# Halving the first transfers and moving the output norms and their turns in a two-block fp32 kernel

## The chip, the cores and the metric

One core of one Trainium2 chip runs the whole program. The metric is device time in microseconds (us), from launch to end, as the median of repeated runs. The engines are TensorE (PE in the rows, PEld for its weight loads), VectorE (DVE), ScalarE (ACT), GpSimd (POOL) and SyncE (SP), each with its own instruction queue, in order, and tied to the others by semaphores. A row's number after L is a line of the kernel.

## The reference

512 tokens of width 1024 pass, in fp32, through three stages, of which this study touches the start of the first and one part of the last.

```python
for i in range(2):                      # first block
    m = even_mixer(x) if i % 2 == 0 else odd_mixer(x)
    x = layer_norm(ALPHA * x + m)
    x = layer_norm(ALPHA * x + square(relu(x @ w_up)) @ w_down)
    x = x + sigmoid(x @ w_gate + b) * (p @ w_proj)
# even_mixer begins with h = x @ w_in; its first 384 columns are c_q
h = rmsnorm(x)                          # second block
q, k, v, g, a, c_b, c_c, c_h = split(h @ w_in_2)
log_a = log_sigmoid(a @ w_gate_up + b_gate) / 16
b = cumsum(log_a) within chunks of 64
q_i, k_i, k_s = q*exp(b), k*exp(-b), k*exp(b_last - b)
o = tril(q_i k_i^T) v + q_i state_prev       # 4 heads, 8 chunks
state = exp(b_last) * state_prev + k_s^T v
o_gla = rmsnorm(o, per head) * g_norm * silu(g)
o_conv = c_b * causal_conv3(c_c * c_h)
x = x + concat(o_gla, o_conv) @ w_out
x = x + (silu(h2 @ w_g) * (h2 @ w_u)) @ w_down ; return rmsnorm(x)
```

## The kernel before

**Products.** Every fp32 operand is held as two parts, H (rounded) and L (the rest), and a product is three matmuls: H with H, H with L, L with H (`mm3`). Weights come as one stream of 303 chunks of 128x1024 (512 KB). SP loads each into one of four raw buffers (`RW`); `cut` on POOL copies it to its H part `WH` (L486) and subtracts to get its L part `WL` (L489), into one of two slots; TensorE waits for `lo_split` before a chunk and raises `chunk_used` after it, which lets POOL cut two chunks on. One chunk against 512 tokens is two steps of k with 12 matmuls each.

**The opening.** ACT's queue loads the transposed input `XS` in four pieces of 512 KB, two steps of k each, and casts each to `XTH`; DVE subtracts to `XTL` (L1207). POOL cuts chunks 0 to 3. TensorE runs 28 matmuls on a tile of ones (`occupy`, operand `IDLE`), whose results nobody reads, then for each of eight k: four token tiles of 384 columns and one tile of 512 columns, three matmuls each, the three parts of a product next to each other. The matmuls of `occupy` keep TensorE at work while it would wait.

**The mixer of the second block.** Its tokens are taken in T = 4 tiles. For tile t the steps on TensorE are `score` (12 matmuls and two turns of `KK`, into banks 4 and 5), `key_values` (banks 6 and 7), `output` (bank 6) and `turn_output` (four turns of `OT` into bank 5, so that it can be multiplied with `w_out`). They are put by hand between the half-chunks of three `features` calls (24 matmuls between two steps), which compute the projections `c_b`... as columns of features in banks 0 to 3. `f(t)` is `turn_output(t)` followed by 11 matmuls of `occupy`, except for the last; `score(0)` has 14 ahead of it.

DVE runs, in order: the three products `QI`, `KI`, `KK` with `QK` (L1628); `operands(0)` (the parts of the two operands, L1634 to L1637, which raise `gla_ops`); then for each t `cut_scores(t)` (mask and parts of the scores, parts of the turned keys, L1645 to L1651, and four casts of the query parts, L1655 and L1656), `operands(t+1)`, `norm_output(t-1)` (L1682 to L1695, with a square root on ACT in the middle), `states(t)` (L1663 to L1673: the parts of the state, twice, and its update, `gla_states` after the second pair of parts), and `output_lo(t-1)` (L1701). After the loop come the convolution's product, its first tap, `norm_output(3)`, the second tap, `output_lo(3)` and the third.

ACT copies finished banks (`copy_banks`), the mixer's outputs (`output_out`), takes the square roots (`output_std`) and casts the turned outputs (`output_hi`), in the order of a loop over t.

The last turn, `f(3)`, stands before the last 24 matmuls of the third `features` call; the product with `w_out` follows and waits for `out_cut` 4.

Of the kernel before, what the change touches and what calls it, by code (L numbers as in the profile page):

```python
# [21 lines left out]
F32 = mybir.dt.float32  # L22
F32R = mybir.dt.float32r
ALU = mybir.AluOpType
ACT = mybir.ActivationFunctionType

P = 128
# [142 lines left out]
def program(nc, d, out):  # L170
    ctx = ExitStack()
    with ctx:
# [166 lines left out]

        landed = [sem(f"raw_landed{j}") for j in range(RAW)]  # L340
        hi_split = sem("hi_split")
        lo_split = sem("lo_split")
# [72 lines left out]
        mix_out = sem("mix_out")  # L415
        gla_ops = sem("gla_operands")
        gla_scored = sem("gla_scored")
        gla_cut = sem("gla_cut")
# [27 lines left out]
        def _(sp):  # L446
# [4 lines left out]

            for j in range(RAW):
                if j >= 2:
                    sp.wait_ge(xs_landed[j - 2], 16)
                load(0, j)
# [22 lines left out]
        def _(pool):  # L478
# [42 lines left out]
            own(pool.memset(ONE[:, :], 1.0))  # L521
            for j in range(RAW):
                cut(0, j)
            over_chunks(pool, RAW, FIRST["out0"], cut)
# [62 lines left out]
        def _(pe):  # L587
# [19 lines left out]

            def features(c, bank, r=0, new=0, freed=None, steps=None):

                columns, k_tiles = (0, P, 2 * P, 3 * P), KD
                for k in range(k_tiles):
                    cc, u = c + k // 2, UNIT * (k % 2)
                    if new:
                        pe.wait_ge(xt_ready, KD * (new - 1) + k + 1)
                    if k % 2 == 0:
                        chunk(cc, r)
                    for m, col in enumerate(columns):
                        if freed is not None and k == 0:  # L620
                            pe.wait_ge(mix_out, freed + m + 1)
                        w = slice(u + col, u + col + P)
                        x = mm3(PS[:, bank + m, :], WH[:, cc % WS, w], WL[:, cc % WS, w],
                                XTH[:, k, :], XTL[:, k, :], k == 0, k == k_tiles - 1)
                    if k % 2:
                        x.then_inc(chunk_used, 1)
                        if steps:
                            for step, t in steps[k // 2]:
                                step(t)
# [289 lines left out]
            pe.wait_ge(idle_made, 1)  # L919
            occupy(1, 28)  # L920
            c = FIRST["cq"]
            for k in range(KD):
                cc, u = c + k // 2, UNIT * (k % 2)
# [188 lines left out]
            def score(t):  # L1112


                if t == 0:
                    occupy(6, 14)
                pe.wait_ge(gla_ops, t + 1)
                if t >= 2:
                    pe.wait_ge(out_cut, t - 1)
                for h in range(GLA_H):  # L1120
                    rows, p = slice(DK * (h % 2), DK * (h % 2 + 1)), h // 2
                    mm3(PS[:, 4 + h % 2, P * p:P * (p + 1)], KIH[rows, p, :], KIL[rows, p, :],
                        QIH[rows, p, :], QIL[rows, p, :], True, True)
                for p in range(2):
                    x = pe.transpose(PS[:, 5, P * (p + 2):P * (p + 3)], KK[:, p, t * P:(t + 1) * P], IDENT[:, :])
# [15 lines left out]
            def output(t):  # L1141

                pe.wait_ge(gla_states, t + 1)
                for p in range(2):
                    w = slice(2 * DV * p, 2 * DV * (p + 1))
# [9 lines left out]
            def turn_output(t):  # L1155

                pe.wait_ge(out_gated, t + 1)
                if t < T - 1:
                    pe.wait_ge(gla_cut, t + 2)
                for f in range(GLA_H):  # L1160
                    x = pe.transpose(PS[:, 5, f * P:(f + 1) * P], OT[:, t, f * P:(f + 1) * P], IDENT[:, :])
                x.then_inc(out_turned, 1)

            s, v, o = score, key_values, output

            def f(t):

                turn_output(t)
                if t < T - 1:
                    occupy(4, 11)  # L1170

            features(c + 12, 0, freed=0, steps=[[], [(s, 0)], [(v, 0)], [(o, 0), (s, 1)]])
            features(c + 16, 0, freed=4, steps=[[(v, 1)], [(f, 0), (o, 1), (s, 2)], [(v, 2)],
                                                [(f, 1), (o, 2), (s, 3)]])
            features(c + 20, 0, freed=8, steps=[[(v, 3)], [(f, 2), (o, 3)], [(f, 3)], []])
            pe.wait_ge(out_cut, 4)
# [14 lines left out]
        def _(ve):  # L1191
# [11 lines left out]
            ve.memset(EPS[:, 1:2], RMS_EPS)  # L1203
            for j in range(4):
                w = slice(2 * j, 2 * j + 2)
                ve.wait_ge(xt_hi, j + 1)
                ve.tensor_tensor(XTL[:, w, :], XS[:, w, :], XTH[:, w, :].bitcast(F32), SUB).then_inc(xt_ready, 2)  # L1207
# [417 lines left out]

            for n, (o, src) in enumerate(((QI, QG), (KI, KG), (KK, KG))):
                ve.wait_ge(gla_act, n + 2)
# [11 lines left out]
            def cut_scores(t):  # L1639
# [11 lines left out]
                ve.tensor_tensor(SML[:, :], SMF[:, :], SMH[:, :].bitcast(F32), SUB).then_inc(gla_cut, 1)  # L1651
                ve.wait_ge(gla_ops, t + 1)
                for e in range(2):
                    k = slice(GCH * e, GCH * (e + 1))
                    ve.tensor_copy(QEH[:, e, :, k], QIH[:, :, k].bitcast(F32))  # L1655
                    x = ve.tensor_copy(QEL[:, e, :, k], QIL[:, :, k].bitcast(F32))  # L1656
                own(x)

# [44 lines left out]

            operands(0)
            for t in range(T):
                cut_scores(t)
                if t < T - 1:
                    operands(t + 1)
                if t:
                    norm_output(t - 1)  # L1710
                states(t)
                if t:
                    output_lo(t - 1)
            ve.wait_ge(mix_out, 12)
            own(ve.tensor_tensor(U[:, :, 2:S + 2], U[:, :, 2:S + 2], CV[:, :, :], M))

# [9 lines left out]
            own(x)  # L1726
            norm_output(T - 1)
            taps(1)
            output_lo(T - 1)
            taps(2)  # L1730
# [13 lines left out]
        def _(act):  # L1744
# [5 lines left out]

            for j in range(4):
                w = slice(2 * j, 2 * j + 2)
                load(XS[:, w, :], d["xt"][:, w, :], xs_landed[j])
            for j in range(4):
                w = slice(2 * j, 2 * j + 2)
                act.wait_ge(xs_landed[j], 16)
                act.copy(XTH[:, w, :], XS[:, w, :]).then_inc(xt_hi, 1)
            load(ONEHOT[:, :], d["onehot"], const_landed)
            load(REL[:, :], d["rel"], const_landed)
# [210 lines left out]
            def copy_banks(o, chunks):  # L1970

                act.wait_ge(chunk_used, chunks)
                for m in range(4):
                    act.copy(o[:, m, :], PS[:, m, :]).then_inc(mix_out, 1)

            def output_out(t):
                act.wait_ge(gla_out, t + 1)
# [10 lines left out]

            c = FIRST["gla"]
            copy_banks(CV, c + 16)  # L1990
            for t in range(T):
                output_out(t)
                output_std(t)
                output_hi(t)
                if t == 1:
                    copy_banks(U[:, :, 2:S + 2], c + 20)
            copy_banks(QK, c + 24)
# [140 lines left out]
```

## Time and profile before

| | us |
|---|---|
| median of 3 runs (2023.68 to 2025.64) | 2023.72 |
| profiled execution, its own time | 2025.68 |
| its span | 2023.9 |
| busy PE / PEld / DVE / ACT / POOL | 1972.5 / 1634.2 / 875.3 / 316.2 / 1272.6 |
| mean granted clock of TensorE | 0.995 |

The span is the time between the first and the last recorded instruction. Matmuls are pipelined: the start of one to the start of the next is what it costs, and its own duration in a row is longer. A matmul of the tile of ones counts as busy. Idle time of an engine is shown ahead of an instruction in brackets, with what ended it.

### The profile page before, as it was taken

How to read it: one execution, taken by the hardware profiler on the slowest of the kernel's cores; microseconds unless marked ns; L12 is line 12 of the kernel's file. 1: busy time of each engine (PE TensorE's matmuls, PEld its weight loads, DVE VectorE, ACT ScalarE, POOL GpSimd, SP SyncE). 2: the span in 40 equal slices, each digit the busy share in tenths (PEclk: the TensorE clock that was granted, in tenths of full speed). 3: DMA queues.
4: the chain of work that ended last, by engine and by line, in shares of the span. 5: the costliest groups of instructions: out<-in, count | busy, mean ns of one | idle time of the engine just before them, and what ended most of it. 6: DMA issues, size and time to landing. Idle time of an engine off the chain costs nothing.

```text
span 2023.9 us, 24676 instructions
## 1 busy us (share of the span) xinstructions
PE 1972.5 (97%) x9253; PEld 1634.2 (81%) x9253; DVE 875.3 (43%) x1215; ACT 316.2 (16%) x601; POOL 1272.6 (63%) x831
## 2 busy tenths in 40 slices
PE   9999999999999999999999999999999899999998
PEld 8778778888887878888788888877887778888886
DVE  3367282343338610472732343377368740000234
ACT  1247120000003100362300000033111130000001
POOL 5488566667775547775566677765553456666675
PEclk9999999999999999999999999999999999999999
DMA  6310323333332223212233333322221223323332
GB/s 213 125 43 1 94 94 95 101 96 114 95 102 83 84 84 95 68 55 76 73 115 102 94 115 95 102 77 80 76 84 53 63 84 95 103 94 93 96 101 73
DMA packets 53410, 181.32 MB, mean 90 GB/s; under 512 B 6552, under 2 KB 9290, under 8 KB 53210
## 3 DMA queue, kind: packets, MB, share of 16 engines
q1 hardware_dynamic: 46512, 165.17, 26.4%
q10 hardware_dynamic: 6826, 15.11, 2.2%
q8 instruction: 54, 0.88, 0.2%
q14 instruction: 18, 0.15, 0.0%
HBM read 176.56 MB, written 3.70 MB: 89 GB/s over the span
## 4 chain that ended last, share of the span: by engine, by line
PE 85%; DVE 9%; POOL 3%; ACT 1%; issue 1%; DMA 0%; POOLq 0%; DVEq 0%
PE PS L589 83%; PE PS L748 1%; POOL WL L489 1%; PE PS L825 1%; DVE OT L1693 1%; DVE STL L1664 1%; POOL WH L486 1%; DVE X L1509 0%; DVE X L1408 0%; DVE PS L1391 0%; POOL PB L518 0%; DVE PTL L1334 0%; DVE ST L1673 0%; POOL AQL L495 0%; POOL AKL L495 0%
## 5 line engine op out<-in xcount | busy, mean ns | idle before, releaser
L489 POOL TENSOR_TENSOR WL<-RW,WH 128x1024 fp32r<-128x1024 f32 x303 | 767.7, 2534 | 25.3
L486 POOL TENSOR_SCALAR WH<-RW 128x1024 fp32r<-128x1024 f32 x303 | 351.4, 1160 | 669.3 <-PE PS L589 640.7
L589 PE MATMUL PS<-XTH,WH 128*128 128x512 f32 x1168 | 458.3, 392 | 2.5 <-DVE XTL L1441 1.6
L589 PE MATMUL PS<-XTL,WH 128*128 128x512 f32 x1168 | 456.2, 391 | 0.0
L589 PE MATMUL PS<-XTH,WL 128*128 128x512 f32 x1168 | 456.0, 390 | 0.0
L589 PE MATMUL PS<-WL,HSH 128*128 128x512 f32 x688 | 267.6, 390 | 2.1 <-POOL WL L489 2.1
L589 PE MATMUL PS<-WH,HSH 128*128 128x512 f32 x688 | 267.7, 389 | 0.0
L589 PE MATMUL PS<-WH,HSL 128*128 128x512 f32 x688 | 267.7, 389 | 0.0
L589 PEld LDWEIGHTS PS<-XTH,WH 128*128 128x128 f32 x1168 | 220.2, 189 | 51.1 <-DVE XTL L1441 3.6
L589 PEld LDWEIGHTS PS<-XTH,WL 128*128 128x128 f32 x1168 | 220.0, 188 | 46.0
L589 PEld LDWEIGHTS PS<-XTL,WH 128*128 128x128 f32 x1168 | 220.1, 188 | 44.8
L589 PE MATMUL PS<-WH,XTH 128*128 128x512 f32 (+1 forms) x480 | 184.7, 385 | 4.4 <-DVE SG L1521 1.8
L589 PE MATMUL PS<-WL,XTH 128*128 128x512 f32 (+1 forms) x480 | 183.4, 383 | 0.5 <-POOL WL L489 0.5
L589 PE MATMUL PS<-WH,XTL 128*128 128x512 f32 (+1 forms) x480 | 183.5, 382 | 0.0
L1494 DVE CAST HSH<-HT 128x512 fp32r (+1 forms) x86 | 40.3, 468 | 273.9 <-PE PS L589 273.1
L589 PEld LDWEIGHTS PS<-WL,HSH 128*128 128x128 f32 x688 | 128.9, 188 | 30.0 <-POOL WL L489 3.4
L589 PEld LDWEIGHTS PS<-WH,HSH 128*128 128x128 f32 x688 | 129.1, 188 | 27.0
L589 PEld LDWEIGHTS PS<-WH,HSL 128*128 128x128 f32 x688 | 129.1, 188 | 26.8
L1495 DVE TENSOR_TENSOR HSL<-HT,HSH 128x512 fp32r<-128x512 f32 x86 | 124.0, 1442 | 3.0
L1456 DVE TENSOR_SCALAR HT<-PS 128x2048 f32 (+1 forms) x16 | 36.7, 2292 | 201.2 <-PE PS L589 200.5
L589 PEld LDWEIGHTS PS<-WH,XTH 128*128 128x128 f32 x480 | 90.1, 188 | 26.0 <-issue 8.3
L1478 DVE TENSOR_TENSOR HT<-PS,GT 128x1024 f32 (+1 forms) x11 | 13.5, 1225 | 214.7 <-ACT GT L2008 214.7
(313 smaller groups left out, 2346.0 us busy)
## 6 DMA issues: line engine op xcount, KB each, us to landing
RW<-stream SPq DMA_DIRECT2D x303, 512.0 KB, 3.6
BC<-gate_rows SPq DMA_DIRECT2D x16, 256.0 KB, 3.2
G<-gain_rows ACTq DMA_DIRECT2D x5, 512.0 KB, 3.5
XS<-xt ACTq DMA_DIRECT2D x4, 512.0 KB, 8.0
X<-x ACTq DMA_DIRECT2D x1, 2048.0 KB, 11.9
G<-bias_vecs ACTq DMA_DIRECT2D x4, 512.0 KB, 5.1
out<-X SPq DMA_DIRECT2D x4, 512.0 KB, 2.6
bias_rows<-QM ACTq DMA_DIRECT2D x1, 1536.0 KB, 6.8
```

What stands on the lines that cost most here:

```text
L486: pool.tensor_scalar(WH[:, j % WS, :], RW[:, j % RAW, :], 1.0, 1.0, ALU.mult, ALU.mult).then_inc(hi_split, 1)
L489: pool.tensor_tensor(WL[:, j % WS, :], RW[:, j % RAW, :], WH[:, j % WS, :].bitcast(F32), ALU.subtract).then_inc(lo_split, 1)
L589: return pe.matmul(o, a, b, start=start, stop=stop)
L748: x = pe.transpose(PSF[:, o:o + P], probs(h)[:, p:p + P], IDENT[:, :])
L825: x = pe.transpose(PS[:, 2 * t + k // 4, P * (k % 4):P * (k % 4 + 1)], src[:, k * P:(k + 1) * P], IDENT[:, :])
L1456: ve.tensor_scalar(h, PS[:, 4 * (g % 2):4 * (g % 2) + 4, :], 0.0, None, MAX).then_inc(relued, 1)
L1478: ve.tensor_tensor(h, PS[:, bank + 2:bank + 4, :], GT[:, :, :], M).then_inc(relued, 1)
L1494: own(ve.tensor_copy(HSH[:, k % 2, :], h))
L1495: ve.tensor_tensor(HSL[:, k % 2, :], h, HSH[:, k % 2, :].bitcast(F32), SUB).then_inc(hs_ready, 1)
L1664: x = ve.tensor_tensor(STL[:, e, :, :], ST[:, :, :], STH[:, e, :, :].bitcast(F32), SUB)
L1693: x = ve.scalar_tensor_tensor(OT[:, t, w], OT[:, t, w], ORS[:, h:h + 1], GN[:, :], M, M)
```

## The change

1. The first weight chunk and the first piece of `XS` are each loaded as two transfers of half the size. ACT, POOL and DVE cut them in halves.
2. The first four k on TensorE are ordered by part: all five H-with-H products of a k (or of k 2 and 3 together), then those with `WL`, then those with `XTL`. The matmuls of `occupy` ahead are 18 in place of 28.
3. The H part of chunk 2 is cast by ACT, ahead of ACT's loads of constants; POOL only subtracts.
4. In the mixer, `KK` is multiplied behind `operands(0)`, with a semaphore of its own (`gla_keys`) that `score(0)` waits for ahead of its two turns. `occupy` ahead of `score(0)` has 6 matmuls in place of 14, and the 33 behind the turns are gone.
5. The four casts of the query parts go from DVE to ACT (`query_parts`); DVE waits for them (`gla_parts`) before it writes the next operands.
6. On DVE `norm_output(t-1)` comes behind `states(t)`, and `output_lo` one tile later. `norm_output(3)` and `output_lo(2)` come ahead of the convolution, and `output_lo(3)` inside its product, which is now four instructions.
7. On TensorE each turn comes one or more steps later; turns 0 to 2 no longer stand directly ahead of `output`, and turn 3 stands after k = 6 of the third `features` call, ahead of its last 12 matmuls. A turn now also waits for the `output_lo` of the tile before.
8. ACT's order is written out by hand.

```diff
@@ -449,7 +454,10 @@
-            for j in range(RAW):
+            sp.dma_start(RW[:, 0, 0:UNIT], d["stream"][0][:, 0:UNIT]).then_inc(half_landed, 16)
+            sp.dma_start(RW[:, 0, UNIT:], d["stream"][0][:, UNIT:]).then_inc(landed[0], 16)
+            for j in range(1, RAW):
@@ -519,8 +527,18 @@
-            for j in range(RAW):
-                cut(0, j)
+            for half, (here, done) in enumerate(((half_landed, half_lo), (landed[0], lo_split))):
+                w = slice(UNIT * half, UNIT * (half + 1))
+                pool.wait_ge(here, 16)
+                pool.tensor_scalar(WH[:, 0, w], RW[:, 0, w], 1.0, 1.0, ALU.mult, ALU.mult).then_inc(hi_split, 1)
+                pool.wait_ge(hi_split, half + 1)
+                pool.tensor_tensor(WL[:, 0, w], RW[:, 0, w], WH[:, 0, w].bitcast(F32),
+                                   ALU.subtract).then_inc(done, 1)
+            cut(0, 1)
+            pool.wait_ge(hi_split, 6)
+            pool.tensor_tensor(WL[:, 0, :], RW[:, 2, :], WH[:, 0, :].bitcast(F32),
+                               ALU.subtract).then_inc(lo_split, 1)
+            cut(0, 3)
@@ -622,6 +640,8 @@
+                    if k == 6 and inner:
+                        inner[0](inner[1])
@@ -917,9 +937,36 @@
-            occupy(1, 28)
+            occupy(1, 18)
             c = FIRST["cq"]
-            for k in range(KD):
+            def opening(k, a, b, first):
+                u = UNIT * (k % 2)
+                for t in range(T):
+                    ts = slice(t * P, (t + 1) * P)
+                    mm(PS[:, 4 + t, 0:Q_LORA], a[:, k, ts], b[:, k // 2, u:u + Q_LORA], first, False)
+                w = slice(u + Q_LORA, u + UNIT)
+                return mm(PS[:, 0, :], b[:, k // 2, w], a[:, k, :], first, False)
+            for ks in ((0,), (1,), (2, 3)):
+                for k in ks:
+                    pe.wait_ge(xt_hi, (1, 2, 3, 3)[k])
+                    pe.wait_ge(hi_split, (1, 2, 4, 4)[k])
+                    opening(k, XTH, WH, k == 0)
+                for k in ks:
+                    if k == 0:
+                        pe.wait_ge(half_lo, 1)
+                    else:
+                        chunk(k // 2)
+                    opening(k, XTH, WL, False)
+                for k in ks:
+                    pe.wait_ge(xt_ready, k + 1)
+                    x = opening(k, XTL, WH, False)
+                if k % 2:
+                    x.then_inc(chunk_used, 1)
+            for k in range(4, KD):
@@ -1113,14 +1160,16 @@
-                    occupy(6, 14)
+                    occupy(6, 6)
                 pe.wait_ge(gla_ops, t + 1)
-                if t >= 2:
-                    pe.wait_ge(out_cut, t - 1)
+                if t >= 3:
+                    pe.wait_ge(out_cut, t - 2)
...
+                if t == 0:
+                    pe.wait_ge(gla_keys, 1)
@@ -1141,6 +1190,7 @@
+                pe.wait_ge(gla_parts, t + 1)
@@ -1156,23 +1206,20 @@
-                    pe.wait_ge(gla_cut, t + 2)
+                    pe.wait_ge(gla_cut, min(t + 3, T))
+                if t:
+                    pe.wait_ge(out_cut, t)
...
-            s, v, o = score, key_values, output
-            def f(t):
-                turn_output(t)
-                if t < T - 1:
-                    occupy(4, 11)
+            s, v, o, f = score, key_values, output, turn_output
             features(c + 12, 0, freed=0, steps=[[], [(s, 0)], [(v, 0)], [(o, 0), (s, 1)]])
-            features(c + 16, 0, freed=4, steps=[[(v, 1)], [(f, 0), (o, 1), (s, 2)], [(v, 2)],
-                                                [(f, 1), (o, 2), (s, 3)]])
-            features(c + 20, 0, freed=8, steps=[[(v, 3)], [(f, 2), (o, 3)], [(f, 3)], []])
+            features(c + 16, 0, freed=4, steps=[[(v, 1)], [(o, 1), (s, 2)], [(f, 0), (v, 2)],
+                                                [(o, 2), (s, 3)]])
+            features(c + 20, 0, freed=8, steps=[[(f, 1), (v, 3)], [(o, 3)], [(f, 2)], []],
+                     inner=(f, 3))
@@ -1201,9 +1248,12 @@
-            for j in range(4):
+            for k in range(2):
+                ve.wait_ge(xt_hi, k + 1)
+                ve.tensor_tensor(XTL[:, k, :], XS[:, k, :], XTH[:, k, :].bitcast(F32), SUB).then_inc(xt_ready, 1)
+            for j in range(1, 4):
                 w = slice(2 * j, 2 * j + 2)
-                ve.wait_ge(xt_hi, j + 1)
+                ve.wait_ge(xt_hi, j + 2)
@@ -1623,7 +1673,7 @@
-            for n, (o, src) in enumerate(((QI, QG), (KI, KG), (KK, KG))):
+            for n, (o, src) in enumerate(((QI, QG), (KI, KG))):
@@ -1649,12 +1699,9 @@
-                ve.wait_ge(gla_ops, t + 1)
-                for e in range(2):
-                    k = slice(GCH * e, GCH * (e + 1))
-                    ve.tensor_copy(QEH[:, e, :, k], QIH[:, :, k].bitcast(F32))
-                    x = ve.tensor_copy(QEL[:, e, :, k], QIL[:, :, k].bitcast(F32))
-                own(x)
+                if t < T - 1:
+                    ve.wait_ge(gla_parts, t + 1)
@@ -1702,17 +1749,25 @@
+            ve.wait_ge(gla_act, 4)
+            ve.tensor_tensor(KK[:, :, :], KK[:, :, :], KG, M).then_inc(gla_keys, 1)
...
+                if t >= 2:
+                    output_lo(t - 2)
+                states(t)
                 if t:
                     norm_output(t - 1)
-                states(t)
-                if t:
-                    output_lo(t - 1)
+            norm_output(T - 1)
+            output_lo(T - 2)
             ve.wait_ge(mix_out, 12)
-            own(ve.tensor_tensor(U[:, :, 2:S + 2], U[:, :, 2:S + 2], CV[:, :, :], M))
+            for f in range(T):
+                if f == 2:
+                    output_lo(T - 1)
+                x = ve.tensor_tensor(U[:, f, 2:S + 2], U[:, f, 2:S + 2], CV[:, f, :], M)
+            own(x)
@@ -1724,9 +1779,7 @@
-            norm_output(T - 1)
             taps(1)
-            output_lo(T - 1)
@@ -1748,13 +1801,22 @@
-            for j in range(4):
+            load(XS[:, 0, :], d["xt"][:, 0, :], xs_half)
+            load(XS[:, 1, :], d["xt"][:, 1, :], xs_landed[0])
+            for j in range(1, 4):
                 w = slice(2 * j, 2 * j + 2)
                 load(XS[:, w, :], d["xt"][:, w, :], xs_landed[j])
-            for j in range(4):
+            for k, here in enumerate((xs_half, xs_landed[0])):
+                act.wait_ge(here, 16)
+                act.copy(XTH[:, k, :], XS[:, k, :]).then_inc(xt_hi, 1)
+            for j in range(1, 4):
...
+            act.wait_ge(landed[2], 16)
+            act.wait_ge(hi_split, 4)
+            act.wait_ge(chunk_used, 1)
+            act.copy(WH[:, 0, :], RW[:, 2, :]).then_inc(hi_split, 2)
@@ -1973,6 +2035,16 @@
+            def query_parts(t):
+                act.wait_ge(gla_ops, t + 1)
+                if t:
+                    act.wait_ge(gla_out, t)
+                for e in range(2):
+                    k = slice(GCH * e, GCH * (e + 1))
+                    act.copy(QEH[:, e, :, k], QIH[:, :, k].bitcast(F32))
+                    x = act.copy(QEL[:, e, :, k], QIL[:, :, k].bitcast(F32))
+                x.then_inc(gla_parts, 1)
@@ -1987,13 +2059,24 @@
+            query_parts(0)
             copy_banks(CV, c + 16)
-            for t in range(T):
-                output_out(t)
-                output_std(t)
-                output_hi(t)
-                if t == 1:
-                    copy_banks(U[:, :, 2:S + 2], c + 20)
+            output_out(0)
+            query_parts(1)
+            output_std(0)
+            output_out(1)
+            query_parts(2)
+            output_hi(0)
+            copy_banks(U[:, :, 2:S + 2], c + 20)
+            output_std(1)
+            output_out(2)
+            query_parts(3)
+            output_hi(1)
+            output_std(2)
+            output_out(3)
+            output_std(3)
+            output_hi(2)
+            output_hi(3)
...

```

## Rows read from the trace of the kernel before

**Rows 1.** The whole span: whom TensorE waited for, one row: us in total, times, longest.

```profile
PE PS L589 <- DVE STL L1664: 4.4, 4, 1.4
```

**Rows 2.** Timeline of TensorE in the opening: start us, us, what, [idle before it].

```profile
1.07 9.27 PE L589 MATMUL PS<-IDLE 128*128 128x512 f32 x28 [1.07 <-DVE IDLE L1201]
11.09 0.41 PE L589 MATMUL PS<-WH,XTH 128*128 128x384 f32 x1 [0.75 <-POOL WL L489]
...
13.95 0.33 PE L589 MATMUL PS<-WH,XTH 128*128 128x384 f32 x1
```

**Rows 3.** Window of the opening: busy us (x instructions) by engine, granted clock, DMA share, GB/s.

```profile
0.00:6.70 6.70, 5.63 (x13) 4.46 (x14) 0.18 (x3) 1.68 (x2) 0.65 (x6) 1.00 0.67 232
```

**Rows 4.** Timeline of GpSimd in the opening, its cuts of chunks 0 and 1.

```profile
6.36 1.06 POOL L486 TENSOR_SCALAR WH<-RW 128x1024 fp32r<-128x1024 f32 x1 [5.51 <-DMA RW<-stream]
7.50 3.45 POOL L489 TENSOR_TENSOR WL<-RW,WH 128x1024 fp32r<-128x1024 f32 x1
...
13.03 3.24 POOL L489 TENSOR_TENSOR WL<-RW,WH 128x1024 fp32r<-128x1024 f32 x1
```

**Rows 5.** Timeline of ScalarE in the opening.

```profile
6.30 1.05 ACT L1757 CAST XTH<-XS 128x1024 fp32r<-128x1024 f32 x1 [2.11 <-DMA XS<-xt]
```

**Rows 6.** Timeline of TensorE in the mixer, ahead of score(0).

```profile
1497.95 3.33 PE L589 MATMUL PS<-IDLE 128*128 128x512 f32 x14
1502.22 0.33 PE L589 MATMUL PS<-QIH,KIH 64*128 64x128 f32 x2 [0.94 <-DVE QIL L1637]
```

**Rows 7.** Timeline of VectorE there.

```profile
1493.62 2.07 DVE L1628 TENSOR_TENSOR KK<-KK,QK 128x1024 f32<-128x1024 f32 x1
...
1499.57 2.60 DVE L1637 TENSOR_TENSOR QIL<-QI,QIH 128x256 fp32r<-128x256 f32 x1
```

**Rows 8.** Timeline of TensorE, one tile's round: starts of the steps from score(3) on.

```profile
1561.02 0.33 PE L589 MATMUL PS<-QIH,KIH 64*128 64x128 f32 x2
...
1562.04 0.47 PE L589 MATMUL PS<-XTH,WH 128*128 128x512 f32 x1
...
1567.68 0.38 PE L589 MATMUL PS<-VH,KTH 64*128 64x256 f32 x1
...
1568.93 0.50 PE L589 MATMUL PS<-XTH,WH 128*128 128x512 f32 x1
...
1574.55 0.60 PE L1161 MATMUL PS<-IDENT,OT 128*128 128x128 f32 x4
1574.90 2.76 PE L589 MATMUL PS<-IDLE 128*128 128x512 f32 x11
1579.08 0.39 PE L589 MATMUL PS<-STH,QEH 128*128 128x256 f32 x1 [1.41 <-DVE STL L1664]
...
1581.89 0.45 PE L589 MATMUL PS<-XTH,WH 128*128 128x512 f32 x1
```

**Rows 9.** Timeline of VectorE: norm_output(1), parts of the state twice, norm_output(3).

```profile
1545.54 0.87 DVE L1682 BATCH_NORM_STATS2 OBN<-OT 128x6 f32<-128x128 f32 x4
...
1552.54 0.69 DVE L1664 TENSOR_TENSOR STL<-ST,STH 128x512 fp32r<-128x512 f32 x1
...
1555.31 2.75 DVE L1664 TENSOR_TENSOR STL<-ST,STH 128x512 fp32r<-128x512 f32 x1
...
1585.15 0.88 DVE L1682 BATCH_NORM_STATS2 OBN<-OT 128x6 f32<-128x128 f32 x4
```

**Rows 10.** Timeline of GpSimd beside the second of those parts.

```profile
1555.09 2.43 POOL L489 TENSOR_TENSOR WL<-RW,WH 128x1024 fp32r<-128x1024 f32 x1
```

**Rows 11.** Timeline of TensorE, the last turn.

```profile
1592.29 1.12 PE L1161 MATMUL PS<-IDENT,OT 128*128 128x128 f32 x4 [4.72 <-DVE OT L1695]
```

**Rows 12.** Windows around an earlier wait and the last turn.

```profile
119.40:122.80 3.40, 1.10 (x5) 0.97 (x6) 3.30 (x2) 3.15 (x2) 3.32 (x3) 1.00 0.01 2
122.80:126.20 3.40, 3.40 (x12) 2.72 (x10) 2.02 (x2) 0.00 (x0) 3.32 (x3) 0.50 0.46 114
...
1590.53:1597.35 6.82, 5.06 (x14) 4.21 (x15) 6.75 (x10) 0.59 (x1) 0.83 (x1) 0.50 0.27 77
```

More of the change, by code:

```diff
@@ L340, in program @@
         landed = [sem(f"raw_landed{j}") for j in range(RAW)]
+        half_landed = sem("first_half_landed")
+        half_lo = sem("first_half_lo")
+        xs_half = sem("first_input_half_landed")
         hi_split = sem("hi_split")
@@ L416, in program @@
         gla_ops = sem("gla_operands")
+        gla_keys = sem("gla_keys")
+        gla_parts = sem("gla_parts")
         gla_scored = sem("gla_scored")
@@ L606, in chunk, with features @@
                     pe.wait_ge(lo_split, c + 1 + r)
-            def features(c, bank, r=0, new=0, freed=None, steps=None):
+            def features(c, bank, r=0, new=0, freed=None, steps=None, inner=None):
                 columns, k_tiles = (0, P, 2 * P, 3 * P), KD
```

## The prediction, made before the change was run

> **What bounds the kernel now.** I read the busy shares first: TensorE is busy 1972.5 of 2023.9 us, so only what stands between its products can move the end. The table of its waits came next, and then the timeline of TensorE in the two places that the diff touches, since a matmul on the tile of ones counts as busy and is in no list of waits.
>
> In the opening TensorE runs 28 such matmuls and then waits 0.75 us for the L part of chunk 0; its first product starts at 11.09, and a step of k costs 13.95 - 11.09 = 2.86 us [rows 2]. Thirteen of the 28 start in the first 6.7 us, about 0.43 us apart; later ones are about 0.23 apart [rows 2, 3].
>
> In the mixer four things cost time. Ahead of score(0) stand 14 such matmuls and 0.94 us of waiting, 1502.22 - 1497.95 = 4.3 us in all [rows 6]. Ahead of output(1), output(2) and output(3) the same picture comes three times, one of which is shown: 11 matmuls and 1.41 us of waiting for the parts of the state, 1579.08 - 1574.90 = 4.2 us [rows 8]; the four waits for those parts sum to 4.4 us [rows 1], so that the wait of output(0), which has no turn ahead, is only about 4.4 - 3 x 1.4 = 0.2. The last turn waits 4.72 us for the normed output [rows 11], and TensorE's clock is then granted at half (1.2 in place of 2.4 GHz) from 1590.5 to 1597.4; TensorE works again from 1592.3, so 5.1 us pass at half and about 2.5 are lost [rows 11, 12].
>
> **The change part by part.**
>
> *Opening.* Eighteen matmuls of ones instead of 28: 13 by 6.7 us and five more at 0.23, so TensorE is free at about 7.8 [rows 2, 3]. Are the halves there by then? The whole first transfer of weights is issued by 0.8 and waited for until 6.36 [rows 4]; half as many bytes should be there between 4.2 and 5 (estimate: between half of those 5.5 us and nearly all of them). The whole piece of the input is cast at 6.30 [rows 5]; its half likewise some 1.5 earlier. The cuts in halves take 0.5 to 0.6 us for H (half of 1.06) and 1.2 to 1.7 for L (half of 2.4, undisturbed, to half of 3.45) [rows 4, 10], the input's cast 0.5 [rows 5]. Half 0 is then ready by about 5.6 (H) and 7.2 (L), half 1, landing as now, by 7.8 and 9.4. TensorE wants its L part only one third into k = 0 and all of k = 1 at 7.8 + 2.9 = 10.7. So nothing waits, and the first product starts 11.09 - 7.8 = 3.3 us earlier. Bounds: 1.5 if the L half is late or the halves land hardly earlier, 3.4 above. Chunk 1's L part ended at 16.27 [rows 4]; it is now wanted behind the H products of k = 2 and 3, at 7.8 + 5.7 + 1.9 = 15.4, and its cut starts some 2 us earlier, at 9, so a margin of about 1 us is left. Reordering matmuls by part costs nothing: their number and shapes stay. For chunk 2, ACT's cast (1.05, as [rows 5]) waits for k = 1 (13.5) and GpSimd's L part follows by 18, ahead of 19.3. Behind that cast ACT's ten small loads of constants and the 2 MB of X start about 2 us later; they are wanted in the next stage, and the margin covers it. Gain 3.3.
>
> *score(0).* Six matmuls instead of 14 end at about 1497.95 + 1.4 = 1499.3. VectorE's product for KK (2.07) moves behind the operands, whose last part ended at 1502.17 [rows 7]; without it and on the near side of GpSimd's cut they end by about 1498.3. The product itself is then ready between 1499.4 and 1500.5, and TensorE wants it 0.9 us into its scores. I take 1499.3 for the start: a gain of 1502.2 - 1499.3 = 2.9. Lower bound 0: if the last part falls behind GpSimd's subtraction, as it does now (2.60 us where it is short), KK is ready only at 1503.
>
> *output(1) to output(3).* The turn leaves the place ahead of each, and with it the 11 matmuls. With norm_output behind states, the parts of the state start when TensorE has made key_values, as they do for output(0); that one waits 0.2. Each of the three therefore gives 4.2 - 0.2, together 12.0. The cover is the 24 matmuls between key_values and output: 1574.55 - 1568.93 = 5.6 us [rows 8]. VectorE needs about as much: the two parts, an update between, and one subtraction of 2.75 that would be 0.69 without GpSimd's 2.43 beside it [rows 9, 10]. So a slip there shows at once. Upper and lower bound: 12.5, and 9 if each slips by one microsecond.
>
> At this place the Trainium skill names the cause of the 2.75: the GPSIMD Engine Reference, Specifications, says that GpSimd shares its SBUF interfaces with VectorE where a VectorE instruction has two SBUF inputs or runs in its two-port mode. By that rule the cut costs VectorE up to 2.4 us once per chunk in whatever is running; by the rows it does so only where instructions happen to meet, and this is in the 5.6 already.
>
> What queues behind? Per round TensorE needs (from score to score, without ones and turn) 1.0 + 5.6 + 1.3 + 5.6 + 2.8 = 16.3 us, plus 0.35 for a turn: 16.7 [rows 8]. VectorE has in the same round the norm (1545.54 to about 1552.1, 6.6 us with a stand for GpSimd), 6 for the states, 2.3 cutting scores, 1.3 operands, 0.7 for output_lo (sums of the timeline from 1559 to 1582): 16.9 at worst, 15 if the norm meets no cut [rows 9]. The four casts (0.7 us a tile) are now ACT's, which is nearly idle. The turns have 24 or more matmuls of slack behind the norm. I count 0 for turns 0 to 2, bound 3.
>
> *The last turn.* After output(3) starts, TensorE comes to it in 2.8 + 5.6 + 0.35 + 2.8 = 11.6 us. VectorE must finish the state's update (1.4), norm_output(2) (5 to 6.6), norm_output(3) (5 to 7.1, since 1585.15 to 1592.2 is the latter with a GpSimd cut beside it) and output_lo(2) (0.7), for which the turn now waits as well: 12.1 to 15.8. I take 14.2, nearer the upper end because a cut starts just there: a wait of 2.6 in place of 4.72, gain 2.1 [rows 9, 11]. The clock's loss of 2.5 goes if that wait leaves the level alone. Waits of 1.4 left it [rows 8]; one of 2.3 us, at 119.4, was followed by 3.4 us at half, a loss of 1.7 [rows 12]. I take 1.8 back of the 2.5.
>
> A rule speaks against this part. The Trainium skill, TensorE: Matmul & The Clock Gate, What's actually happening, says that the gate falls to half on an idle engine and opens only after activity. By it each removed run of ones risks a fall. The trace agrees where a wait is 2.3 or 4.7 and not at 1.4.
>
> *Convolution.* It now starts behind norm_output(3). TensorE wants its last part four chunks (22 us) into the next product, and about 17 us of VectorE work remain: hidden.
>
> **Sum.** 3.3 + 2.9 + 12.0 + 2.1 + 1.8 = 22.1 us. The profiled execution took 2025.68, its span 2023.9; it is 2 us above the median shown. On its own time the sum gives 2003.6, on the median 2023.72 - 22.1 = 2001.6; I say 2002.
>
> **Rivals.**
> - *VectorE stays the bound* (0.22). Its round of up to 16.9 us against TensorE's 16.7, every slip met by a cut of 2.4. For it: VectorE is nearly full here. Against: four casts leave it. Turns and outputs then wait 1 to 2.4 us in each of three rounds and the last turn 4: 6 us given back, 2008.
> - *KK comes late* (0.12): score(0) waits for it to 1503 and the first 2.9 are gone: 2005.
> - *The halves give nothing* (0.05): transfers of half the size land no earlier, or a later load is wanted: 1.5 or less of the 3.3: 2004.
> - *No wait at the last turn* (0.06): norms that never meet a cut: 1999.
> - *Not faster* (0.03): with 51 matmuls of ones gone, the waits left each pull the clock down and it stays at half. At half, a microsecond of products costs another. The stage's 80 us then become 102, and the gain of 22 is gone, when 44 of them run at half; two thirds of it at half would make it 120 and give 2042. Against: rows at full clock around every wait of 1.4. [...]
>
> The forecast has 0.52.
>
> **Range and chances.** Below, 1998 takes the best case and the noise of 2 us that the three runs show; above, 2009 takes VectorE as the bound. 0.2% (4 us) is what a measurement of this kernel can tell from no change. Faster than 2019.7: all cases but the last, 0.96; within 4 us 0.02; slower 0.02.
>
> **What the next profile would show.** First product on TensorE at 7.8, not 11.1. score(0) at 1.4 us after the products before it. Waits before output(1) to output(3) under 0.5 us each and no ones between turn and output. The last turn waiting under 3 us, for output_lo(2) or the norm. VectorE busy throughout, ACT with 16 small casts of about 0.25 us. The stage from the ones ahead of score(0) to the product with w_out 19 us shorter. It goes wrong if VectorE's norms reach past the turns (PE then waits for OT or OL in every round), if the KK product stands behind a cut, or if half clock shows outside the last turn.

## The result and the profile after

The changed kernel takes 2006.2 us (2005.45 to 2008.23, four runs) where the kernel before took 2024.36 in the same comparison: 18.2 us less, a ratio of 0.9912 with a 95% interval of 0.9899 to 0.9926. The forecast was 2002 and a gain of 22.1. Three executions of the kernel before, made beside the experiments below, took 3291 to 4774 us and are left out of every comparison.

The profiled execution took 2006.85 us. From its page, the span and the busy time of each engine:

```profile
span 2004.9 us, 24589 instructions
...
PE 1959.3 (98%) x9202; PEld 1624.1 (81%) x9202; DVE 872.9 (44%) x1203; ACT 320.5 (16%) x619; POOL 1271.8 (63%) x832
```

The span is 19.0 us shorter, and TensorE is busy 13.2 us less. The change takes out 51 matmuls of ones (10 + 8 + 33), which at 0.23 us each are 11.7 of it.

**The opening.** TensorE, from the ones on, grouped by what is multiplied (x4: the four token tiles):

```profile
1.07 6.65 PE L607 MATMUL PS<-IDLE 128*128 128x512 f32 x18 [1.07 <-DVE IDLE L1248]
7.56 0.86 PE L607 MATMUL PS<-WH,XTH 128*128 128x384 f32 x4
...
8.48 0.86 PE L607 MATMUL PS<-WL,XTH 128*128 128x384 f32 x4
...
9.42 0.86 PE L607 MATMUL PS<-WH,XTL 128*128 128x384 f32 x4
...
10.35 0.86 PE L607 MATMUL PS<-WH,XTH 128*128 128x384 f32 x4
```

The first product starts at 7.56 in place of 11.09 [rows 2], the three parts follow each other without a wait, and k = 1 begins at 10.35. GpSimd's cuts over the same time:

```profile
5.15 0.62 POOL L533 TENSOR_SCALAR WH<-RW 128x512 fp32r<-128x512 f32 x1 [4.31 <-DMA RW<-stream]
5.85 1.82 POOL L535 TENSOR_TENSOR WL<-RW,WH 128x512 fp32r<-128x512 f32 x1
...
8.85 1.29 POOL L535 TENSOR_TENSOR WL<-RW,WH 128x512 fp32r<-128x512 f32 x1
...
11.25 3.25 POOL L497 TENSOR_TENSOR WL<-RW,WH 128x1024 fp32r<-128x1024 f32 x1
```

GpSimd waits for the first half until 5.15, where it waited for the whole chunk until 6.36 [rows 4]. The L part of that half is there at 7.7 and wanted at 8.5. The L part of chunk 1 ends at 14.5 and is wanted at 15.0, a margin of 0.5 us where the forecast had about 1. At k = 4 TensorE is 3.6 us earlier than before.

**Ahead of score(0).**

```profile
1493.46 1.52 PE L607 MATMUL PS<-IDLE 128*128 128x512 f32 x6
1494.91 0.34 PE L607 MATMUL PS<-QIH,KIH 64*128 64x128 f32 x2
```

The scores start 1.45 us after the first of the ones, not 4.3 [rows 6], and there is no wait. VectorE, for the same place:

```profile
1490.49 2.50 DVE L1686 TENSOR_TENSOR KIL<-KI,KIH 128x256 fp32r<-128x256 f32 x1
1492.92 0.41 DVE L1687 TENSOR_TENSOR QIL<-QI,QIH 128x256 fp32r<-128x256 f32 x1
1493.26 1.21 DVE L1753 TENSOR_TENSOR KK<-KK,QK 128x1024 f32<-128x1024 f32 x1
```

The operands end at 1493.3, and the product for KK takes 1.21 us and ends at 1494.5. The turns that want it start at 1495.7.

**TensorE's waits, whole span.** Three rows of the table, each with us in total, times, longest. They answer to [rows 1] and [rows 11]; the waits for OL and XTL are new:

```profile
PE PS L1213 <- DVE OL L1748: 2.6, 1, 2.6
...
PE PS L607 <- DVE XTL L1789: 2.3, 1, 2.3
...
PE PS L607 <- DVE STL L1711: 0.6, 2, 0.3
```

The waits for the parts of the state sum to 0.6 us, not 4.4: 0.28 each ahead of output(0) and output(1), none ahead of the others. The last turn waits 2.59 us, not 4.72, and, as forecast, for output_lo(2). The wait of 2.3 us for XTL of L1789 was not forecast: it is the L part of the convolution's output, ahead of chunk 4 of the product with w_out.

**Behind the last turn.** Windows around the wait for XTL (the granted clock is the third figure from the end):

```profile
1599.00:1603.30 4.30, 1.97 (x9) 1.31 (x8) 3.29 (x5) 0.62 (x1) 3.00 (x2) 1.00 0.40 122
1603.30:1606.80 3.50, 3.50 (x11) 2.72 (x10) 0.00 (x0) 0.00 (x0) 1.23 (x1) 0.51 0.25 53
```

Behind this wait TensorE runs at half clock for 3.4 us. Behind the last turn, where [rows 12] show half clock for 6.8 us, it now stays at full. VectorE over the same time:

```profile
1577.38 4.61 DVE L1780 TENSOR_SCALAR CV<-U,CW 128x512 f32<-128x512 f32 x4
1582.03 11.43 DVE L1775 SCALAR_TENSOR_TENSOR CV<-U,CW,CV 128x512 f32<-128x512 f32 x8
1593.49 5.55 DVE L1786 TENSOR_TENSOR CV<-CV,QK 128x512 f32<-128x512 f32 x4
1598.97 3.33 DVE L1789 TENSOR_TENSOR XTL<-CV,XTH 128x512 fp32r<-128x512 f32 x4
```

The convolution's work takes from 1573.9 to 1602.3, 28.4 us. In it lie output_lo(3) (0.69 us) and a wait of 0.23 ahead of it, so some 27.4 are the convolution's own.

**The stage as a whole.** From the ones ahead of score(0) to the first product with w_out TensorE now takes 1577.37 - 1493.46 = 83.9 us; before it took 1600.60 - 1497.95 = 102.65. That is 18.7 us less, and the forecast said 19.

In each round VectorE stands idle for 1.0 to 3.1 us ahead of output_lo or the parts of the state. The forecast had it busy throughout, and this sign did not show.

### The profile page after: what moved, and what is told of

It is laid out like the page before. It is cut to its first block, busy times and chain, and to the rows that moved or that the text cites. A ratio compares the mean times of both kernels' runs of the same rounds, so it can differ in the third digit from the quotient of the medians.

```text
span 2004.9 us, 24589 instructions
## 1 busy us (share of the span) xinstructions
PE 1959.3 (98%) x9202; PEld 1624.1 (81%) x9202; DVE 872.9 (44%) x1203; ACT 320.5 (16%) x619; POOL 1271.8 (63%) x832
## 4 chain that ended last, share of the span: by engine, by line
PE 87%; DVE 7%; POOL 3%; ACT 1%; issue 1%; POOLq 0%; DVEq 0%
PE PS L607 85%; PE PS L768 1%; POOL WL L497 1%; PE PS L845 1%; POOL WH L494 1%; DVE CV L1775 1%; DVE X L1559 0%; DVE STL L1711 0%; DVE X L1458 0%; DVE PS L1441 0%; POOL PB L526 0%; DVE PTL L1384 0%; POOL AQL L503 0%; POOL AKL L503 0%; ACT PTH L1889 0%
```

## The experiments

Eleven kernels were run, each beside the kernel before on the same chip. The medians of the kernel before lie between 2023.8 and 2025.0 us, so medians of different groups can differ by 1 us for no reason of the kernel, and ratios are the better comparison. The intervals reach 0.10% to 0.18% to either side, 2 to 3.6 us. A smaller difference between two of these kernels can't be told from the times, and there the traces decide. One trace of each kernel was kept.

| run | median us | ratio | interval |
|---|---|---|---|
| the changed kernel | 2006.2 | 0.9912 | 0.9899 to 0.9926 |
| opening only | 2021.2 | 0.9985 | 0.9975 to 0.9995 |
| mixer only | 2009.2 | 0.9925 | 0.9907 to 0.9942 |
| convolution by chunk | 2003.3 | 0.9898 | 0.9880 to 0.9916 |
| ones out only | 2030.9 | 1.0022 | 1.0005 to 1.0038 |
| last turn in bank 4 | 2003.0 | 0.9896 | 0.9880 to 0.9913 |
| casts on VectorE | 2006.9 | 0.9911 | 0.9894 to 0.9927 |
| keys first | 2009.2 | 0.9931 | 0.9914 to 0.9947 |
| norm before states | 2033.5 | 1.0043 | 1.0029 to 1.0057 |
| by product | 2003.5 | 0.9891 | 0.9874 to 0.9909 |
| whole transfers | 2005.7 | 0.9902 | 0.9885 to 0.9920 |
| fewer ones | 2000.7 | 0.9876 | 0.9858 to 0.9893 |

**1 and 2. The two halves of the change.** The first has the five pieces of the opening from the diff and nothing else; the second has all the rest.

> The kernel before with the change's opening alone (halved transfers, 18 matmuls of ones, products by part, ScalarE's cast of chunk 2); the mixer as before. Theory (the two parts add, and the opening gives what its first product gains, 11.09 - 7.56 = 3.5 us): 2020.8 against 2024.3. Rival (the opening's gain is lost again later, to constants that land 2 us later or to a clock that falls elsewhere): 2023 to 2025, with a longer wait of VectorE for SINK or a new half-clock stretch.

> The changed kernel with the opening of before; the mixer as changed. Theory (additive): the mixer gives 18.2 - 3.5 = 14.7, so 2009.6. It is made of 19 or so up to the product with w_out, less the 2.3 us of waiting for the convolution's L part and 1.7 of half clock behind it. Rival: with the opening undone the cuts meet VectorE elsewhere and the wait for the convolution vanishes: 2006 or less.

The opening alone gives 3.6 us by the medians (2024.8 to 2021.2) and 3.0 by the ratio, the mixer alone 15.6 and 15.2. The first was expected at 3.5, the second at 14.7. They add, within the noise, to the 18.2 of the whole. The wait for XTL (2.34 us) and the half clock behind it stand in the mixer alone as well.

**3. The convolution's tiles waited for one by one.** The changed kernel with

```diff
-            pe.wait_ge(conv_lo, 4)
             for k in (4, 5):
+                pe.wait_ge(conv_lo, k - 3)
                 wide(c + k, 0, XTH[:, k, :], XTL[:, k, :], False)
+            pe.wait_ge(conv_lo, 4)
```

> The changed kernel, but TensorE waits for the convolution's tiles one by one (tile f ahead of chunk 4 + f of the product with w_out, tile 3 with tile 2) and not for all four ahead of chunk 4. Theory (the term that the prediction missed is this wait of 2.33 us and the 3.4 us at half clock behind it, 1.7 lost): 2006.2 - 4.0 = 2202.2 less 200, that is 2002.2; no wait for XTL in the table, no half clock there. Rival (the tiles come so slowly that the wait returns ahead of tile 1 or 3): 2004.5 or more. Second rival (the clock's fall is tied to the last turn's 2.6 us wait and merely came late): the wait goes, the half clock stays, 2003.9.

(The figure meant there is 2002.2.) Measured 2003.3, ratio 0.9898 against 0.9912. Two of TensorE's waits between 1480 and 1625:

```profile
PE PS L1213 <- DVE OL L1749: 2.6, 1, 2.6
PE PS L607 <- DVE STL L1712: 0.5, 2, 0.3
```

and the clock over the last turn and the product with w_out:

```profile
1565.00:1625.00 60.00, 56.72 (x257) 45.71 (x255) 44.43 (x52) 13.41 (x25) 33.44 (x19) 1.00 0.24 72
```

The wait for XTL is gone and none has taken its place. The clock stays at full, although the last turn still waits 2.6 us; that speaks against the second rival. By the trace the missed term is 2.33 us of waiting and 1.7 of half clock, 4.0 in all. By the medians it is 3.0 and by the ratios 2.8, with intervals that overlap, so its size rests on the trace.

**4. Only the matmuls of ones out.** The kernel before with

```diff
-                    occupy(6, 14)
+                    occupy(6, 6)
...
-                if t < T - 1:
-                    occupy(4, 11)
```

> The kernel before with the matmuls of ones in the mixer taken out alone (6 in place of 14 ahead of score(0), none behind the turns); every order as before. Theory (the ones only filled a wait that VectorE's order makes; the gain comes from the order): no gain, the waits ahead of output(1) to output(3) grow from 1.4 to about 4 us, and the clock falls behind some of them, 1.7 us each: 2024 to 2030. Rival (the ones themselves were the cost): 41 x 0.23 = 9.4 us gained, 2015.

It got slower: 2030.9, ratio 1.0022. Eight of its ten runs took 2027.9 to 2032.5. The other two took 2020.7 and 2020.9, some 3.5 us less than the kernel before. Their mean granted clock is 0.992, and so is that of the run of 2027.9, so the clock alone does not explain them; why they differ is open. TensorE's waits in the mixer, in a run of 2031:

```profile
PE PS L589 <- DVE STL L1662: 8.0, 3, 3.9
PE PS L1161 <- DVE OT L1693: 5.4, 1, 5.4
PE PS L589 <- DVE QIL L1635: 2.7, 1, 2.7
```

and three windows of it:

```profile
1499.12:1505.95 6.83, 6.83 (x26) 5.64 (x27) 4.19 (x13) 0.00 (x0) 0.00 (x0) 0.50 0.22 79
1536.67:1546.91 10.24, 9.73 (x44) 9.01 (x45) 4.72 (x11) 0.58 (x1) 0.00 (x0) 0.50 0.17 51
1560.56:1574.22 13.66, 11.74 (x49) 10.53 (x50) 8.06 (x23) 1.20 (x3) 1.31 (x1) 0.50 0.13 38
```

What the ones had filled is now waiting (8.0 us for the parts of the state, 3.9 at the longest, 2.7 ahead of score(0)), and with the waits the clock is at half for 6.8, 10.2 and 13.7 us, and for some more behind the last turn. In this trace the ones cost nothing where they stood: TensorE would have waited. What made it wait was VectorE's order, as the runs 7 and 8 show.

**5. The last turn in bank 4.** The kernel of 3, with bank 4 for the last turn, on TensorE, ScalarE and VectorE, and

```diff
-                if t:
+                if t and t < T - 1:
                     pe.wait_ge(out_cut, t)
+                bank = 4 if t == T - 1 else 5
```

> As the run with the convolution's tiles waited for one by one (2003.3), and the last turn goes to bank 4, so that it no longer waits for output_lo(2) but for the normed output alone. In the changed kernel output_lo(2) ended 0.7 us behind the norm. Theory: the wait at the last turn is 1.9 in place of 2.6, 2002.6, and its releaser is OT. Rival (the wait is for output_lo in a longer chain): 1 us or more gained. Either is near the noise of the times; the wait in the trace decides.

```profile
1573.44 0.66 PE L1214 MATMUL PS<-IDENT,OT 128*128 128x128 f32 x4 [1.78 <-DVE OT L1744]
```

TensorE waits 1.78 us for OT, 0.8 less than for OL and 0.1 less than expected. The time moves by 0.3 us, which the runs can't tell from nothing.

**6. The casts on VectorE again.** The changed kernel with the four casts in `cut_scores`, as before, and without `query_parts` and its waits.

> The changed kernel with the four casts of the query parts on VectorE again, behind the scores' parts, as before. Theory (VectorE stands idle 1 to 3 us in each round ahead of the states, so 0.7 us more per round is hidden except behind the last norms, where nothing of it stands): 2006.2, at most 2007. Rival (VectorE is the bound, and each cast shows, with a cut of GpSimd that it then meets): 0.7 to 2.4 in each of three rounds, 2008.3 to 2013.

2006.9, ratio 0.9911: no difference that the times can show. In the trace the waits for the parts of the state are 0.8 us in all in place of 0.6, the longest 0.3, and those for OL and XTL are as they were. Part 5 of the change is worth next to nothing here; VectorE had the room.

**7. The product for KK first.** The changed kernel with

```diff
-            operands(0)
             ve.wait_ge(gla_act, 4)
             ve.tensor_tensor(KK[:, :, :], KK[:, :, :], KG, M).then_inc(gla_keys, 1)
+            operands(0)
```

> The changed kernel with the product for KK ahead of operands(0) again. Theory (the 2.9 us ahead of score(0) come from this order and from the ones that the late operands had covered): score(0) starts 2.8 us later, with a wait of that size for QIL, 2009.0. Rival (only the fewer ones count): no later start, 2006.2.

```profile
PE PS L607 <- DVE QIL L1687: 2.7, 1, 2.7
```

Measured 2009.2, 3.0 us more than the changed kernel by the medians and 3.8 by the ratios, with intervals that overlap. The trace shows 2.7 of them in that one wait, of the size expected. The clock stays at full behind it.

**8. The norm ahead of the states.** The changed kernel with

```diff
-                states(t)
                 if t:
                     norm_output(t - 1)
+                states(t)
```

> The changed kernel with norm_output(t-1) ahead of states(t) on VectorE again; TensorE's order stays. Theory (what made output(1) to output(3) wait is the norm ahead of the states): each waits about 4 us for the parts of the state, 12 us in all, and the clock falls behind some of them, 1.7 to 3.4 each: 2018 to 2028, so most or all of the mixer's gain is gone. Rival (the turns' new places alone give the gain): under 2 us each, 2006 to 2010.

```profile
PE PS L607 <- DVE STL L1711: 18.4, 4, 9.1
PE PS L607 <- DVE XTL L1789: 4.8, 1, 4.8
```

```profile
1527.28:1564.82 37.54, 26.98 (x123) 23.41 (x123) 16.95 (x43) 4.21 (x11) 7.69 (x5) 0.68 0.13 42
```

Measured 2033.5, 5 us beyond the theory's upper end. The waits for the states are 18.4 us, not 12, and in the 37.5 us of the window the granted clock is 0.68 on average. Two of the waits are 4.3 and 4.7 us, the size expected. One is 9.1 us long, because here another order bites: norm_output(1) needs a square root that stands on ScalarE behind `copy_banks(U)`, which waits for the chunk that TensorE is at (ScalarE stood 6.4 us for it). VectorE, at that square root:

```profile
1547.78 0.16 DVE L1735 TENSOR_TENSOR OMV<-OMV 128x4 f32<-128x4 f32 x1
1553.70 0.18 DVE L1737 RECIPROCAL ORS<-OSTD 128x4 f32<-128x4 f32 x1 [5.76 <-ACT OSTD L2054]
```

So the run shows that the order of norm and states decides. How much of its 27 us comes from ScalarE's order, which was written for the other order of VectorE, was not measured; the long wait is some 4.6 us above its neighbours.

**9 and 10. The opening's order and its halves apart.** Both from the kernel of 3. In the first, k = 0 to 3 take each product's three parts next to each other; in the second the transfers and cuts of chunk 0 and of the first input piece are whole again.

> As the run that waits for the convolution's tiles one by one (2003.3), with the first four k taken product by product (three parts next to each other) in place of by part. Theory (the order matters only where a part is late: at k = 2, whose L part of chunk 1 ended at 14.5 while TensorE comes at 13.2): a wait of 1.3 us ahead of k = 2, none at k = 0 or 1, 2004.6. Rival (the order matters from the first product): a first product later than 7.9 us and 2 us or more lost, 2005.5.

> As the run that waits for the convolution's tiles one by one (2003.3), with the first transfers and their cuts whole again; order by part and 18 matmuls of ones stay. Theory (the halves are what lets the L part of k = 0 be there by 7.7; whole, it ended at 10.95): H products of k = 0 at about 7.6, then a wait of 2.3 to 2.5 us for the L part, 2005.7. Rival (order by part and fewer ones would have done it): less than 1 us, 2003.8.

TensorE in the first:

```profile
1.07 5.76 PE L607 MATMUL PS<-IDLE 128*128 128x512 f32 x18 [1.07 <-DVE IDLE L1239]
7.77 0.41 PE L607 MATMUL PS<-WH,XTH 128*128 128x384 f32 x1 [0.94 <-POOL WL L535]
...
14.39 0.41 PE L607 MATMUL PS<-WH,XTH 128*128 128x384 f32 x1 [0.81 <-POOL WL L497]
```

and in the second:

```profile
11.15 0.97 PE L596 MATMUL PS<-WL,XTH 128*128 128x384 f32 x4 [2.22 <-POOL WL L492]
```

By product, TensorE waits 0.94 us ahead of k = 0 (its 18 ones took 5.76 us and not 6.65) and 0.81 ahead of k = 2. k = 4 starts at 20.1, 1.3 us later than in the changed kernel (18.8). The time, 2003.5, is not to be told from 2003.3, so the order by part is worth 1.3 us in the trace and none that the times can show.

With whole transfers the H products of k = 0 go through, and their L products wait 2.22 us, as expected; k = 4 starts at 21.5, 2.8 us later than in the changed kernel. Its time, 2005.7, is 2.2 us above that of by product, run beside it, with intervals that overlap. So by the traces the halves give the larger part of the opening's 3.6 us.

**11. Fewer ones.** The kernel of 5, with

```diff
-                if t == 0:
-                    occupy(6, 6)
...
-            occupy(1, 18)
+            occupy(1, 14)
```

> As the run with the last turn in bank 4 (2003.0), without the six matmuls of ones ahead of score(0), whose operands were ready 1.5 us before these ended, and with 14 in place of 18 ahead of the first product, whose first parts were ready 1.8 us before. Theory: 1.3 us at score(0), at most a short wait for KK there, and 0.3 to 0.8 in the opening: 2001.2. Rival (the clock needs them): a fall to half behind one of the two places, 1.7 lost, 2002.9 or more.

```profile
1494.31 0.39 PE L607 MATMUL PS<-XTH,WL 128*128 128x512 f32 x1
1494.63 0.34 PE L607 MATMUL PS<-QIH,KIH 64*128 64x128 f32 x2
```

```profile
19.00 0.41 PE L607 MATMUL PS<-WH,XTH 128*128 128x384 f32 x1 [0.54 <-POOL WL L539]
```

score(0) starts 0.32 us behind the start of the last product before it. In the changed kernel that product starts at 1493.23 and score(0) at 1494.91, 1.68 later: 1.4 gained. In the opening the products start at 7.03 but then wait 0.54 us for the L part of chunk 2, and k = 4 starts at 19.00, where the kernel of 5 has it at 18.78: nothing gained. 2000.7 us, ratio 0.9876, is the lowest of all, and its interval lies wholly below that of the changed kernel; it overlaps with that of the kernel of 5. The trace accounts for 1.2 of the 2.2 us between the two medians. No half clock follows either place.

## Why the forecast was right, and by how much it missed

Direction and range held, and so did the mechanism term by term, except for one. The third column is read from the two traces:

| step | forecast, us | traces before and after, us | run that bears on it |
|---|---|---|---|
| first product | 3.3 | 11.09 to 7.56: 3.5 | opening only, 3.6 |
| score(0) | 2.9 | 4.27 to 1.45: 2.8 | keys first, a wait of 2.7 back |
| outputs 1 to 3, with turns 0 to 2 | 12.0 | 11.4; waits of 0.28, 0, 0, no ones | ones out only; norm before states |
| last turn | 2.1, a wait of 2.6 | 2.1; 2.59, for OL | bank 4: 1.78, for OT |
| clock behind it | 1.8 of 2.5 | 2.4: full clock throughout | convolution by chunk: full at 2.6 us |
| convolution | 0, hidden | -4.2: 2.5 around the wait, 1.7 of clock | convolution by chunk |

The 11.4 compares the times from score(0) to TensorE's arrival at the last turn, less the 12 matmuls that now stand ahead of that turn.

*The step that failed* is the one that called the convolution hidden: "about 17 us of VectorE work remain". The deadline was right: four chunks behind the start of the product, TensorE came at 1599.86, which is 25.9 us after the work began. The work was mis-sized: it took 28.4 us. The prediction does not say what its 17 is made of, and it is short even of the rows of the kernel before: there the same work with output_lo(3) sums to 20.7 us (2.28 for the product, 1.67 for the first tap, 5.46 for the eight instructions of the second and third tap, 5.08, 5.54 and 0.69). With 20.7 the work would still have been hidden. What made the wait is that the taps slowed; the product and the last two steps together did not. In the kernel before they ran where GpSimd stood still, with no cut between 1591.4 and 1601:

```profile
1592.15 2.73 DVE L1720 SCALAR_TENSOR_TENSOR CV<-U,CW,CV 128x512 f32<-128x512 f32 x4
...
1595.52 2.73 DVE L1720 SCALAR_TENSOR_TENSOR CV<-U,CW,CV 128x512 f32<-128x512 f32 x4
```

Moved behind norm_output(3), the same taps lie beside the product with w_out, where GpSimd cuts a chunk every 5.6 us and takes some 3.8 of them:

```profile
1583.36 1.06 POOL L494 TENSOR_SCALAR WH<-RW 128x1024 fp32r<-128x1024 f32 x1 [2.04 <-PE PS L607]
1584.50 2.71 POOL L497 TENSOR_TENSOR WL<-RW,WH 128x1024 fp32r<-128x1024 f32 x1
1588.98 1.13 POOL L494 TENSOR_SCALAR WH<-RW 128x1024 fp32r<-128x1024 f32 x1 [1.77 <-PE PS L607]
```

Four of the eight instructions of the second and third tap in the trace after, one by one:

```profile
1582.70 0.74 DVE L1775 SCALAR_TENSOR_TENSOR CV<-U,CW,CV 128x512 f32<-128x512 f32 x1
1583.36 1.58 DVE L1775 SCALAR_TENSOR_TENSOR CV<-U,CW,CV 128x512 f32<-128x512 f32 x1
1584.87 2.88 DVE L1775 SCALAR_TENSOR_TENSOR CV<-U,CW,CV 128x512 f32<-128x512 f32 x1
1587.79 0.75 DVE L1775 SCALAR_TENSOR_TENSOR CV<-U,CW,CV 128x512 f32<-128x512 f32 x1
```

The first and the last of these meet no cut and keep their 0.75 us. The second meets GpSimd's copy of 1583.36 and the third its subtraction of 1584.50, and each ends half a microsecond behind the end of the cut that it met. All eight follow this: four of 0.75 us, two of 1.5 to 1.6, two of 2.9. They took 11.43 us in place of 5.46, and the first tap 4.61 in place of 1.67. So the slowing is shown instruction by instruction, though not by a run without the cuts, which was not made.

[rows 10] had shown what a cut does to one instruction, and the prediction used it for the states and not for the convolution. The Trainium skill (GPSIMD Engine Reference, Specifications) says that GpSimd shares its SBUF interfaces with VectorE and that VectorE instructions with two SBUF inputs, or in a two-port mode, contend with it. The taps have two SBUF inputs, and the trace agrees: they rise from 0.75 to 2.9 us.

*The sum.* In the traces the opening gives 3.6 us, the stage 18.7 and the convolution takes back 4.2, which makes 18.1; the spans differ by 19.0, and the 0.9 left over lies between the opening and the mixer, where the diff changes nothing. The forecast had 3.3 and 18.8. That its sum less the 4.0 of experiment 3 is 18.1, against 18.2 between the medians, is partly luck, since runs of one kernel spread by 2 to 3 us.

*The rival that did not come.* "VectorE stays the bound" was given 0.22. Casts on VectorE shows how far it was: with the four casts back on it (0.7 us a tile by the forecast), the waits for the states in the rounds stayed at 0.3 us or less. VectorE was the bound in two other places: at the last turn, as forecast, and behind the rounds, which the rival did not name.

*The fall of the clock.* The Trainium skill (TensorE: Matmul & The Clock Gate, What's actually happening) says that the clock is at half on an idle engine and that activity releases it. The traces agree in direction. With the ones out and the order kept, waits of 2.7 to 5.4 us came with 31 us at half clock in the three windows shown, and a slower kernel. In this part of the changed kernel the waits left the clock at full but for one, of 2.33 us.

The length of the wait does not decide alone. The last turn's wait of 2.56 to 2.59 us left the clock at full in all seven traces that have it. The wait of 2.32 to 2.34 us for XTL was followed by half clock in all four that have it. Ahead of score(0), 2.70 us left it at full in keys first, and 2.69 us came with half clock in ones out only. No run settles which waits the clock passes over. The forecast's 1.8 was a guess between the two outcomes, and that it came close is luck.

## What to carry to other kernels

Filler work ahead of a wait can be a sign of an order that makes the wait: change the order first, then take the filler out. Filler alone taken out made this kernel slower in eight runs of ten. The new order with all the filler kept was not run. When work is moved on an engine, size it by rows from the place it goes to, with the neighbours it will have there, not by rows from the place it leaves. And a wait for the last of several pieces is worth splitting into waits for each, as soon as the pieces come close to their deadline: here that removed a wait of 2.33 us.

## What the runs showed of the hardware

- The convolution's tap instructions, which read two tiles in SBUF, end about half a microsecond behind a cut of GpSimd that they meet: one of 128x512 takes 0.75 us alone, 1.5 to 1.6 beside GpSimd's copy and 2.9 beside its subtraction. Eight in a row took 11.43 us against 5.46, with cuts in 3.8 of every 5.6 us.
- In the changed kernel a wait of 2.33 us was followed by 3.4 us at half clock, one of 2.59 us some 28 us earlier by none. The 4.72 us of the kernel before came with 6.8 us at half.
- ScalarE's cast of 128x128, not in the trace before, takes 0.30 us, and four follow each other every 0.20 us. VectorE's took 0.22, every 0.14.
